# Three-pass products stream their moving rows backwards and write their banks backwards

## The reference

```python
def sq_relu_mlp(h, w1, w2):
    a = jax.nn.relu(h @ w1)
    return (a * a) @ w2
...
zxbcdt = u @ w_in
...
q, fz, v, g = jnp.split(u @ w_in, 4, axis=-1)
...
x = h + jax.nn.sigmoid(h @ ple_w_gate[i]) * (p[i] @ ple_w_proj[i])
```

## Time and profile before

| | us |
|---|---|
| median of 3 runs | 1888.76 |
| lowest and highest | 1887.98 and 1889.18 |
| the profiled execution | 1887.8 |
| its span, first to last instruction | 1885.9 |
| TensorE (PE) busy | 1860.2 |
| VectorE (DVE) busy | 1139.6 |
| ScalarE (ACT) busy | 922.0 |
| GpSimd (POOL) busy | 178.1 |

### The profile page before, as it was taken

The page is one execution under the profiler, slowest core; times in us unless marked ns, Lnnn a source line. Parts: engine busy times, 40 slices in busy tenths (PEclk is TensorE's granted clock), DMA queues, the critical chain, the costliest instruction groups (busy, mean ns, idle before and its releaser), DMA issues.

```text
span 1885.9 us, 26981 instructions
## 1 busy us (share of the span) xinstructions
PE 1860.2 (99%) x9678; PEld 1572.5 (83%) x9678; DVE 1139.6 (60%) x2013; ACT 922.0 (49%) x1827; POOL 178.1 (9%) x137
## 2 busy tenths in 40 slices
PE   8999999999999999999999999999999999999998
PEld 7788787877888888899999977888888889887987
DVE  5677677557443434557887876634444587556765
ACT  5765765453332324546768655323333364535551
POOL 0201202004000000400101003100000220001100
PEclk9999999999999999999999999999999999999999
DMA  6131214314233222313312124323222222320001
GB/s 200 45 108 41 76 45 157 112 68 156 89 108 115 90 89 90 89 46 90 91 45 67 46 81 143 112 90 115 106 89 89 90 101 93 117 101 1 1 0 45
DMA packets 116738, 162.02 MB, mean 86 GB/s; under 512 B 6085, under 2 KB 57251, under 8 KB 116643
## 3 DMA queue, kind: packets, MB, share of 16 engines
q1 hardware_dynamic: 115347, 156.04, 24.8%
q0 software_dynamic: 1296, 4.72, 0.7%
HBM read 158.64 MB, written 2.10 MB: 85 GB/s over the span
## 4 chain that ended last, share of the span: by engine, by line
PE 92%; DVE 4%; ACT 3%; DVEq 1%; issue 0%; ACTq 0%; DMA 0%; SPq 0%
PE psum L907 52%; PE psum L702 15%; PE psum L1081 8%; PE psum L667 4%; PE psum L1114 3%; PE psum L1344 2%; PE psum L853 1%; PE psum L940 1%; DVE arena L2275 1%; DVE z_lo L2199 1%; PE psum L1001 1%; PE psum L860 1%; PE psum L848 1%; ACT rn L1548 1%; ACT arena L1542 0%; PE psum L1188 0%
## 5 line engine op out<-in xcount | busy, mean ns | idle before, releaser
L2432 DVE TENSOR_TENSOR w_lo<-slot,w_hi 128x512 fp32r<-128x512 f32 x304 | 232.9, 785 | 352.7 <-ACT w_hi L1654 352.6
L1654 ACT CAST w_hi<-slot 128x512 fp32r<-128x512 f32 x304 | 185.4, 623 | 426.0 <-PE psum L907 410.5
L907 PE MATMUL psum<-f_lo,w_hi 128*128 128x512 f32 x528 | 205.4, 389 | 0.0
L907 PE MATMUL psum<-f_hi,w_hi 128*128 128x512 f32 x512 | 199.8, 390 | 1.4 <-DVE f_lo L2480 1.0
L907 PE MATMUL psum<-w_hi,hid_hi 128*128 128x512 f32 x512 | 199.5, 390 | 0.0
L907 PE MATMUL psum<-w_hi,hid_lo 128*128 128x512 f32 x512 | 199.2, 389 | 0.0
L907 PE MATMUL psum<-w_lo,hid_hi 128*128 128x512 f32 x512 | 199.2, 389 | 0.0
L907 PE MATMUL psum<-f_hi,w_lo 128*128 128x512 f32 x512 | 199.2, 389 | 0.0
L3056 POOL TENSOR_TENSOR res<-rn,gb 128x1024 f32<-128x1024 f32 x16 | 46.2, 2888 | 838.5 <-DVE rn L2420 632.5
L907 PEld LDWEIGHTS psum<-f_lo,w_hi 128*128 128x128 f32 x528 | 99.1, 188 | 20.5 <-issue 0.2
L907 PEld LDWEIGHTS psum<-f_hi,w_hi 128*128 128x128 f32 x512 | 96.1, 188 | 22.9 <-DVE f_lo L2480 1.8
(11 more groups left out here) (388 smaller groups left out, 4376.1 us busy)
## 6 DMA issues: line engine op xcount, KB each, us to landing
slot<-in_w_mlp SPq DMA_DIRECT2D x128, 512.0 KB, 5.7
slot<-in_w_ssd SPq DMA_DIRECT2D x32, 512.0 KB, 5.8
slot<-in_w_hgrn SPq DMA_DIRECT2D x32, 512.0 KB, 6.7
slot<-in_w_ssd_out SPq DMA_DIRECT2D x16, 512.0 KB, 6.0
slot<-in_w_gate SPq DMA_DIRECT2D x16, 512.0 KB, 5.4
gb<-in_w_ssd SPq DMA_DIRECT2D x8, 512.0 KB, 7.9
slot<-in_w_hgrn_out SPq DMA_DIRECT2D x8, 512.0 KB, 5.8
slot<-in_w_mla SPq DMA_DIRECT2D x8, 512.0 KB, 5.3
```

The source lines that it names most:

```text
L907: m = pe.matmul(psum[:, bank[c], cols or slice(0, width)], a, m_, start=opens and k == 0 and n_pass == 0, stop=closes and k == KD - 1 and ...
L1654: act.copy(w_hi[:, k, :], as_k(slot_of(stage, n))[:, k, :]).then_inc(high_made, 1)
L2432: dve.tensor_tensor(w_lo[:, k, :], as_k(slot_of(stage, n))[:, k, :], w_hi[:, k, :].bitcast(F32), ALU.subtract).then_inc(low_made, 1)
```

## The change

In both functions the moving operand is sliced with step -1, so that TensorE reads its columns from the last to the first, and the output is sliced with step -1 too, so that each result goes to the same place in the bank as before, the last column first. The stationary operand, the flags that open and close a sum, and all waits and increments are untouched. A PSUM bank that is filled by one of these two functions is filled in this order by all of its products.

```diff
             def passes(out, still, moving, first, last):
 
                 for n_pass, (a, m_) in enumerate(((still[0], moving[0]), (still[0], moving[1]), (still[1], moving[0]))):
-                    m = pe.matmul(out, a, m_, start=first and n_pass == 0, stop=last and n_pass == 2)
+                    m = pe.matmul(out[:, ::-1], a, m_[:, ::-1], start=first and n_pass == 0, stop=last and n_pass == 2)
                 return m
...
                         for n_pass, (a, m_) in enumerate(((still_hi, moving_hi), (still_hi, moving_lo), (still_lo, moving_hi))):
-                            m = pe.matmul(psum[:, bank[c], cols or slice(0, width)], a, m_, start=opens and k == 0 and n_pass == 0,
+                            m = pe.matmul(psum[:, bank[c], cols or slice(0, width)][:, ::-1], a, m_[:, ::-1], start=opens and k == 0 and n_pass == 0,
                                           stop=closes and k == KD - 1 and n_pass == 2)
```

## The result

The changed kernel takes 1921.88 us (median of 4 runs, 1921.37 to 1923.4) against 1888.37 us for the kernel before: a ratio of 1.018, 95% interval 1.0167 to 1.0193, 33.5 us slower. (Executions of the kernel before spread from 1888 to 1891 us, so the difference is good to about a microsecond.) The forecast was 1888.8 us with a range of 1884 to 1910 us, so it missed.

A forecast was written before the change was run, and what follows sets the result against it. TensorE, busy 1860.2 of 1885.9 us, was taken as the bound; every part of the change was put at 0, leaving the median at 1888.8 us, with a range of 1884 to 1910 us.

The forecast's parts named there:

- Instructions: The two reversed slices on lines 907 and 702 add no product, weight load, semaphore or DMA: 6060 x 0.
- readers: ScalarE and VectorE take whole banks after the bank's last product, so column order moves them neither earlier nor later: 0.
- waits: Semaphores such as `blocks_begun` and `units_begun` hang on whole instructions, so what waits behind them moves only with the products.
- weight loads: The stationary operand isn't turned; its 188 ns load runs beside the stream of the product before: 0.
- the question over the rule on PSUM patterns: Whether a bank write with step -1 counts as non-contiguous, which would slow matmuls; the rule gives no figure.
- The stream itself: Reading and writing columns backwards on lines 907 and 702, the open cost: taken as 0, bounded at 1191 us.
- a price above 3.4 ns: Dearer start beyond line 940's left-over time per product, so a kernel above 1909.4 us: 2%.
- Half rate: Rival: descending columns of the moving read or bank write each take their own access; 1191 us more, 3080 us; 15%.
- A dearer start: Rival: rate stays, each backward row's first access costs extra; 21 us (1909.4) up to 83 us (1972); 11%.
- its larger part: Start cost above 3.4 ns a product, between 21 and 83 us, 1909.4 to 1972 us: 2%.
- Faster: Rival: the 13.7 ns per product shrink as row ends and beginnings lie differently; at most 62 us, 1827 us; 4%.
- My argument from step 0 on the load side: Line 780's load rereads one column yet takes 188 ns like adjacent columns, so a step other than one shows no penalty.

The follow-up runs named there:

- experiment 3: Only the banks written backwards, in both functions of the kernel before, moving rows read forwards: 1889.29 us, ratio 1.0001.
- experiment 1: Separate kernel of product streams on TensorE alone, varying order and width: 512 columns forward 227.1 ns, both operands turned 233.3, moving rows alone 233.3, bank alone 227.1.
- experiment 5: Second streams-only kernel, stationary block shifted, narrowed or broadcast: forward 512-column products took 233.3 ns at 4 columns off, 227.1 at 64 off.
- experiment 7: Kernel before with both functions reading and writing columns in descending blocks of 128, ascending within: 1889.08 us, ratio 0.9998.
- experiment 8: Kernel before, nothing turned, stationary block taken 8 columns beside its place in both MLPs' 1536 up products: 1898.61 us, ratio 1.005.
- The map at 384 columns: Streams-only kernel of 384-column products, varying row start, direction and an 8-column shift of the stationary block: turned rows spread from 175.6 to 180.0 ns.
- the 32-column load: Streams-only kernel with 32 stationary columns loaded instead of 128: load 109 ns instead of 188, forward products 231.5 ns, turned 233.3.

## Why the prediction was wrong

**What held.** TensorE was the bound, with no cover for a slower product: 34.3 us on two lines became 34.0 us of span. Instructions, readers, waits and weight loads cost 0, as put. The split of a product's time into a stream of 0.4167 ns a column and a fixed part of 13.7 ns was the right frame: the loss went into the second part. The bank written backwards cost nothing (experiment 3), which answers, for a step of -1 in fp32, the question over the rule on PSUM patterns in "PSUM — Partial Sum Buffer" of the Trainium skill, Specifications: a step of -1 is not a non-contiguous pattern in its sense, or the rule would have shown here.

**The step that failed** is "The stream itself", where I took 0. The reason given was that a backward row touches the same aligned words as often as a forward one. The rule of the Trainium skill on SBUF lines ("Advanced Engine Details and Errata", Memory Cachelines) doesn't save it. Its lines of 16 bytes are four of these columns. The order inside such a group is free, as that rule has it (227.1 ns, experiment 1), but I took it to say that the order of the groups is free too, and blocks of 4 in descending order cost the full 6.4 ns. The term that I put at 0 measured 6.4 ns at 512 columns: the fixed part of 13.7 ns grew to some 20 (233.5 - 213.3 = 20.2). I gave just 2% to a price above 3.4 ns. That limit came from the plain fp32 row of line 940, a kind of product whose spacing turned out the same in either direction (429.2 ns, experiment 5); it bounded nothing about the start of a three-pass product.

**The rivals.** Half rate didn't happen. "A dearer start" came nearest in kind, and its larger part held the time (33.5 us lies between its 21 and its 83), but that is luck, for it is wrong as told: its price isn't a constant of the backward row. It is +6.4 ns at 512 columns and a gain of 1.7 at 256; it vanishes with descending blocks of 128 (experiment 7), and a forward row pays it too when its stationary partner stands elsewhere (experiments 5 and 8). "Faster" came true for one width alone, 256 columns. My argument from step 0 on the load side, the only row that spoke for the forecast, was a misreading: it looked at the duration of the load, which stayed at 188 ns in the shifted streams as well, while the spacing of the products changed. With that very pattern, one stationary column broadcast, a forward stream follows at 231.7 ns instead of 226.7 (experiment 5).

**What replaces it.** Shown: at one fp32r column per cycle the fixed part of a product depends on the addresses of both SBUF operands, the moving row and the stationary block. In the program of the kernel before, the split operands' tensors and slices lie multiples of 128 columns from one another, and most of its forward rows meet the cheap case (not the attention scores, though they lie so too). Turned rows of 512 and 384 columns don't. So the cause of the loss is shown as far as the order in which groups of columns of the moving row are read. What happens inside the chip is open. Not settled either: which pairs of places are cheap. The map at 384 columns refuted both rules that I had, and the row turned within blocks of 16 columns, the blocks in ascending order, at 12.80 us for 48 or 266.7 ns, fits no pattern of the others. That the two operands' reads share something is what experiments 5 and 8 suggest. The Trainium skill's "TensorE: Matmul & The Clock Gate", Part 2, gives TensorE two independent read ports, so that loading the next weights doesn't steal SBUF read bandwidth from the running product. No run here shows the ports; the 9.3 us of experiment 8 show that the stationary block's place does slow the products, and what the two reads share is open; that it isn't the duration of the load is what the 32-column load suggests. A stream with no loads between its products would tell more; it wasn't tried.

## What to carry to other kernels

Where products run back to back at one column per cycle, look at start-to-start distances, not durations, and take off the stream: what is left (13.7 ns here, 83 us or 4.4% of the span over the 6060 products) is the part that layout moves, by 4 to 13 ns a product in most of the streams here. For fp32r products of 512 and 384 columns, start both SBUF operands at multiples of 64 columns, which was the cheap case here (forward 227 and 173.5 ns). Don't take that for a rule: 448 columns took 202.7 ns from column 64 and 200.2 from 16, in the same kernel. Measure the widths that you use, and test a shifted stationary block as well as a shifted moving row. An unknown that multiplies by thousands of instructions deserves a range from its own size (half of the fixed part was some 41 us), not from a row of another kind.

## What the runs showed of the hardware

- Writing a PSUM bank from its last column to its first costs nothing: 227.1 ns a product, and 1889.29 us for the kernel, as before.
- Reading a moving row backwards costs 6.4 ns at 512 fp32r columns, 4.2 at 384, nothing at 320, and gains 1.6 at 256. At 448 both orders take 206.5 ns from column 0, already some 20 over the stream; at 128 both take 111 to 112 ns, twice the stream.
- What costs at 512 columns is the descending order of groups of columns: blocks of 2, 4, 16 or 32 in descending order take 233 ns, blocks of 64, 128 or 256 take 227. Turned only within pairs or groups of 4, the row takes 227 ns; within groups of 32, 64 or 128 it takes 233; within groups of 16, 266.7.
- Shifting the stationary block by 4 columns costs a forward 512-column product the same 6.4 ns, and one broadcast column 5.0; in the kernel, 8 columns' shift in 1536 products cost 9.3 us.
- Bfloat16 products of 512 columns follow at 215.8 ns and of 384 at 162.5, only 2.5 ns over their stream, whatever the order (at 512) or the places (at 384); plain fp32 ones take 429.2 ns per record both ways. The 13.7 ns, and their sensitivity to place, belong to the fp32r products alone among the kinds tried here.
